# Input projections as seven half-size products for each pair of column blocks, and the program rewritten around such pairs

## The reference, cut to what matters

```python
for i in range(DEPTH):                                   # layer A, then layer B
    q, k, v, mq, gate = split_proj(x @ w_in[i], SPLIT)   # A: 5120 columns, B: 10240 columns
    o_mix = mixer_a(q, k, v, sink, pos) or mixer_b(q, k, v, pos)
    o_mem = memory_attention(mq, mem, w_mkv[i])          # 4 heads, 256 memory tokens
    y = concat([o_mix, o_mem]) * silu(gate)              # 1024 x 2048
    x = layer_norm(ALPHA * x + y @ w_out[i], ln_g[i], ln_b[i])
```

## Time and profile before

| | us |
|---|---|
| median of 3 runs | 2400.32 (2396.41 to 2400.34) |
| profiled execution | 2399.52 |
| its span, first to last instruction | 2397.7 |
| TensorE busy | 2320.9 (97%) |
| VectorE busy | 1375.1 (57%) |
| ScalarE busy | 997.1 (42%) |
| GpSimd busy | 269.4 (11%) |

### The profile page before, as it was taken

The page is one execution under the profiler, slowest core; times in us unless marked ns, Lnnn a source line. Parts: engine busy times, 40 slices in busy tenths (PEclk is TensorE's granted clock), DMA queues, the critical chain, the costliest instruction groups (busy, mean ns, idle before and its releaser), DMA issues.

```text
span 2397.7 us, 37763 instructions
## 1 busy us (share of the span) xinstructions
PE 2320.9 (97%) x11856; PEld 1943.2 (81%) x11856; DVE 1375.1 (57%) x3528; ACT 997.1 (42%) x2329; POOL 269.4 (11%) x214
## 2 busy tenths in 40 slices
PE   8999999999999989999999999999999999999996
PEld 7788888888888877887888788887887878888885
DVE  3455646565443755566565765656656666464375
ACT  4343434344442233443534435344354453444222
POOL 0001000000000221011011110111101111000022
PEclk9999999999999999999999999999999999999998
DMA  7211121211125531112022120221212112122543
GB/s 223 72 45 45 36 62 35 62 35 53 52 97 197 179 132 53 40 51 78 26 71 62 35 71 27 71 62 35 71 29 68 62 35 73 36 86 96 198 174 130
DMA packets 184656, 183.83 MB, mean 77 GB/s; under 512 B 16260, under 2 KB 156620, under 8 KB 183052
## 3 DMA queue, kind: packets, MB, share of 16 engines
q1 hardware_dynamic: 184588, 183.03, 23.9%
HBM read 157.39 MB, written 25.61 MB: 76 GB/s over the span
## 4 chain that ended last, share of the span: by engine, by line
PE 77%; DVE 12%; issue 4%; ACT 4%; DMA 1%; DVEq 0%; POOL 0%; SPq 0%; POOLq 0%; ACTq 0%
PE bank L857 15%; PE bank L859 15%; PE bank L858 15%; PE bank L919 7%; PE bank L894 6%; PE bank L984 5%; PE bank L990 4%; PE bank L988 4%; PE bank L907 4%; DVE work L1369 3%; DVE work L1465 2%; DVE work L1367 2%; DMA w_raw<-in_w_mkv 1%; DVE work L1372 1%; ACT w_split L1092 1%
## 5 line engine op out<-in xcount | busy, mean ns | idle before, releaser
L857 PE MATMUL bank<-xT,w_split 128*128 128x512 f32 (+1 forms) x2048 | 890.8, 435 | 12.8 <-DVE w_split L1337 6.5
L859 PE MATMUL bank<-xT,w_split 128*128 128x512 f32 (+1 forms) x2048 | 789.8, 386 | 0.0
L858 PE MATMUL bank<-xT,w_split 128*128 128x512 f32 (+1 forms) x2048 | 789.6, 386 | 0.0
L857 PEld LDWEIGHTS bank<-xT,w_split 128*128 128x128 f32 x2048 | 390.9, 191 | 75.8 <-DVE xT L1345 7.5
L859 PEld LDWEIGHTS bank<-xT,w_split 128*128 128x128 f32 x2048 | 386.7, 189 | 79.4
L858 PEld LDWEIGHTS bank<-xT,w_split 128*128 128x128 f32 x2048 | 391.4, 191 | 69.1 <-issue 23.5
L1337 DVE TENSOR_TENSOR w_split<-w_raw,w_split 128x1024 fp32r<-128x1024 f32 x200 | 257.4, 1287 | 326.1 <-ACT w_split L1092 163.2
L1125 ACT ACTIVATE work<-work,soft 128x256 f32<-128x256 f32 (+2 forms) x448 | 226.4, 505 | 389.2 <-DVE soft L1401 324.5
L788 POOL TENSOR_TENSOR work<-work,cosb 32x512 f32<-32x512 f32 x128 | 173.1, 1352 | 1421.1 <-ACT work L1182 1342.8
L1182 ACT COPY work<-bank 128x512 f32<-128x512 f32 x176 | 102.7, 584 | 399.0 <-PE bank L859 398.1
L919 PEld LDWEIGHTS bank<-work 128*128 128x128 f32 x1488 | 224.7, 190 | 33.5
(11 more groups left out here) (98 smaller groups left out, 2543.3 us busy)
## 6 DMA issues: line engine op xcount, KB each, us to landing
w_raw<-in_w_in_b SPq DMA_DIRECT2D x80, 512.0 KB, 3.8
w_raw<-in_w_out SPq DMA_DIRECT2D x64, 512.0 KB, 3.4
w_raw<-in_w_in_a SPq DMA_DIRECT2D x40, 512.0 KB, 3.9
work<-weight_scratch SPq DMA_DIRECT2D x12, 1536.0 KB, 6.5
y_scratch<-work SPq DMA_DIRECT2D x32, 512.0 KB, 3.1
y_raw<-y_scratch SPq DMA_DIRECT2D x64, 256.0 KB, 3.5
w_raw<-in_w_mkv SPq DMA_DIRECT2D x16, 512.0 KB, 4.4
work<-in_x SPq DMA_DIRECT2D x4, 1024.0 KB, 7.1
```

Source lines behind the costliest of these rows:

```text
L857: nc.tensor.matmul(dst, w_h, xT[:, 0, k, cols], start=(k == 0), stop=False)
L858: nc.tensor.matmul(dst, w_h, xT[:, 1, k, cols], start=False, stop=False)
L859: return nc.tensor.matmul(dst, w_l, xT[:, 0, k, cols], start=False, stop=(k == KT - 1))
```

## The change

The projection of a pair of column blocks (256 columns) for all 1024 tokens is a product of 2x2 blocks: token halves by halves of the contraction, times halves of the contraction by the two column blocks. Before, it takes eight block products, each 4 contraction steps. Now it takes seven (Winograd's form of Strassen's algorithm), of sums of the activations and sums of the weights:

- **Steps.** A pair is 28 steps, 7 products of 4, where two segments were 32 steps. There are 20 pairs in layer A and 40 in layer B, and the step is the same three matmuls.
- **Activations.** `x_ops` holds seven 512x512 operands, split, where `xT` held four. The sums are made from rows once for each layer (`token_sums`, VectorE and GpSimd), and 28 groups of transposes take the place of 16. In layer A, 24 of them stand in the memory projection; in layer B they stand before the first products (`X_BEFORE`).
- **Weights.** Four quarters of 128x512 are loaded for each pair and seven operands made of them: three sums on VectorE, one on GpSimd, seven casts and seven subtractions of 512 columns where there were two of each of 1024.
- **Results.** Products accumulate in the two banks `PB`: in the first bank the products 0, 2, 4 and 6 on top of each other, in the second 1 and 3, then 5. After the products 0, 1, 2 and 6 ScalarE copies the bank out, after 3, 4 and 5 VectorE adds it to what was copied. A product waits for the reader of the product two before it, since both use the same bank.
- **Riders.** A tile starts every second step, one job rides on one pair. Scores of layer A and of memory heads are plain float32 now. In layer B the normalisation of the tiles is gone (the denominators enter the mixing weights). The sine product is GpSimd's; the minimum of negated logits takes the place of the maximum, without the one-column operation behind it.
- **Mixing** in layer B is done by halves of the tokens, weights loaded by halves.
- **Output projection**: the same matmuls. The first tiles of y are loaded when all of y has been stored.
- The program has no loops.

The diff, cut to its core:

```diff
-STEPS = 2 * KT
-LEAD, LAG_T, LAG_PV = 3, 6, 8
+PRODUCTS = 7
+STEPS = 4 * PRODUCTS
+RAW, RING, AHEAD = 6, 4, 3
+LAG_MASK, LAG_EXP, LAG_NORM, LAG_T, LAG_PV, LAG_OUT = 1, 2, 3, 5, 7, 8
...
-        xT = sb("xT", [P, 2, KT, L], F32R)
-        w_split = sb("w_split", [P, 2, 2, D], F32R)
-        w_raw = sb("w_raw", [P, 2, D])
+        x_ops = sb("x_ops", [P, X_OPS * XW], F32R)
+        raw = sb("raw", [P, RAW, HALF])
+        sums = sb("sums", [P, 2, HALF])
+        ring = sb("ring", [P, RING, 2, HALF], F32R)
...
-            def step(dst, cols, slot, k):
-                w_h = w_split[:, slot, 0, k * P:(k + 1) * P]
-                w_l = w_split[:, slot, 1, k * P:(k + 1) * P]
-                nc.tensor.matmul(dst, w_h, xT[:, 0, k, cols], start=(k == 0), stop=False)
-                nc.tensor.matmul(dst, w_h, xT[:, 1, k, cols], start=False, stop=False)
-                return nc.tensor.matmul(dst, w_l, xT[:, 0, k, cols], start=False,
-                                        stop=(k == KT - 1))
+            def three_parts(dst, n, k, x_h, x_l, start, stop, again=False):
+                w_h = ring[:, n % RING, 0, k * P:(k + 1) * P]
+                w_l = ring[:, n % RING, 1, k * P:(k + 1) * P]
+                nc.tensor.matmul(dst, w_h, x_h, start=start, stop=False, skip_group_check=again)
+                nc.tensor.matmul(dst, w_h, x_l, start=False, stop=False, skip_group_check=again)
+                return nc.tensor.matmul(dst, w_l, x_h, start=False, stop=stop,
+                                        skip_group_check=again)
+                if j == 0 and not first:
+                    pe.wait_ge(c11_done, g)
+                if j == 1 and not first:
+                    pe.wait_ge(c21_done, g)
+                if j >= 2:
+                    pe.wait_ge((r1_done, r5_done, r2_done, c12_done, c22_done)[j - 2], g + 1)
+            def product_step(g, j, k):
+                dst = PB[(g + (j in (1, 3, 5))) % 2][:, :]
+                mm = three_parts(dst, stage_of(g, j), k, xs[:, j, 0, k, :], xs[:, j, 1, k, :],
+                                 start=(k == 0 and j in (0, 1, 5)),
+                                 stop=(k == KH - 1), again=True)
+                if k == KH - 1:
+                    mm.then_inc(prod, 1)
...
+        def x_source(j, i):
+            first, second = slice(0, HALF), slice(HALF, D)
+            return (rows[:, i, first], t1_rows[:, i, :], t2_rows[:, i, :], rows[:, 4 + i, second],
+                    t3_rows[:, i, :], rows[:, i, second], t1_rows[:, i, :])[j]
+        X_BEFORE = (((6,), (), (), (), (), (), ()),
+                    ((0,), (1, 2), (3,), (4,), (5, 6), (), ()))
...
+                if due is not None and due[1] < 3:
+                    (first_sum, second_sum, third_sum)[due[1]](due[0])
+            def first_sum(g):
+                if g > 0:
+                    dve.wait_ge(w_lo, stage_of(g - 1, 2) + 1)
+                    dve.wait_ge(s4_done, g)
+                nc.vector.tensor_tensor(sums[:, 0], quarter(g, 0), quarter(g, 1), ALU.add
+                                        ).then_inc(s1_done, 1)
+            def second_sum(g):
+                dve.wait_ge(w_lo, stage_of(g, 1) + 1)
+                nc.vector.tensor_tensor(sums[:, 0], sums[:, 0], quarter(g, 2), ALU.subtract
+                                        ).then_inc(s2_done, 1)
+            def third_sum(g):
+                dve.wait_ge(s1_done, g + 1)
+                nc.vector.tensor_tensor(raw[:, load_of(g, 0) % RAW], quarter(g, 2), quarter(g, 0),
+                                        ALU.subtract).then_inc(s3_done, 1)
+            def fourth_sum(g):
+                load = load_of(g, 3)
+                pool.wait_ge(s2_done, g + 1)
+                pool.wait_ge(raw_in[load % RAW], landed_value(load))
+                if g > 0:
+                    pool.wait_ge(w_lo, stage_of(g - 1, 3) + 1)
+                nc.gpsimd.tensor_tensor(sums[:, 1], raw[:, load % RAW], sums[:, 0], ALU.subtract
...
+            def summed(g, e, h, j, bank_, before, done):
+                dest = pairs[g].dests[e]
+                dve.wait_ge(*product_done(g, j))
+                dve.wait_ge(before, g + 1)
+                for view, take in dest.views(h):
+                    st = nc.vector.scalar_tensor_tensor(
+                        out=view, in0=take(bank_[:, :]), scalar=dest.factor,
+                        in1=take(r5) if e else view, op0=ALU.mult, op1=ALU.add)
...
+                    pair = pair_at(layer, T, 16)
+                    if pair is not None:
+                        summed(pair.g, 0, 1, 3, PB[1 - pair.g % 2], r2_done, c12_done)
+                    pair = pair_at(layer, T, 20)
+                    if pair is not None:
+                        if pair.g == FIRST_PAIR[1]:
+                            dve.wait_ge(rows_out, 16 * TILES)
+                        if pair.g == FIRST_PAIR[1] + 5:
+                            dve.wait_ge(spilled, 16)
+                        summed(pair.g, 1, 1, 4, PB[pair.g % 2], r5_done, c22_done)
+                    pair = pair_at(layer, T, 24)
+                    if pair is not None:
+                        summed(pair.g, 0, 0, 5, PB[1 - pair.g % 2], r1_done, c11_done)
+                    if T < STEPS and T % 4 == 0:
+                        for op in X_BEFORE[layer][T // 4]:
...
+                    pair = pair_at(layer, T, 4)
+                    if pair is not None:
+                        first_part(pair.g, 0, 0, r1_done)
+                    pair = pair_at(layer, T, 8)
+                    if pair is not None:
+                        fifth_part(layer, pair.g)
+                    pair = pair_at(layer, T, 12)
+                    if pair is not None:
+                        first_part(pair.g, 1, 2, r2_done)
+                    pair = pair_at(layer, T, STEPS)
+                    if pair is not None:
+                        last_part(pair.g)
...
+        if ropes == [0]:
+            self.ropes = [(0, 1, 17, 21), (0, 0, 25, 29)]
+        elif ropes == [0, 1]:
+            self.ropes = [(0, 1, 17, 20), (1, 1, 21, 24), (0, 0, 25, 28), (1, 0, 29, 32)]
...
-                nc.vector.stream_shuffle(b, v, swap).then_inc(rope_turned, 1)
-                dve.wait_ge(rope_turned, r + 1)
-                nc.vector.tensor_tensor(b, b, sin_h, ALU.mult).then_inc(rope_sine, 1)
-                dve.wait_ge(rope_sine, r + 1)
-                dve.wait_ge(rope_cosine, r + 1)
-                nc.vector.tensor_tensor(v, a, b, ALU.add).then_inc(rope_done, 1)
...
+                pool.wait_ge(rope_turned, rope_no[key] + 1)
+                for view, take in dest.views(h, ROPE):
+                    nc.gpsimd.tensor_tensor(view, view, take(cosb[:, h * HALF:(h + 1) * HALF]),
+                                            ALU.mult)
+                for view, take in turned_views(dest, h):
+                    mul = nc.gpsimd.tensor_tensor(view, view, take(sinb[:, h * HALF:(h + 1) * HALF]),
+                                                  ALU.mult)
+                mul.then_inc(rope_mul, 1)
...
+                dve.wait_ge(rope_mul, rope_no[key] + 1)
+                for (view, _), (b, _) in zip(dest.views(h, ROPE), turned_views(dest, h)):
+                    add = nc.vector.tensor_tensor(view, view, b, ALU.add)
+                add.then_inc(rope_done, 1)
...
-                load_w(0, 0, 0)
-                load_w(0, 0, 1)
-                for j in range(3):
-                    sp.wait_ge(stored[j], 16 * totals[j] + (16 if j > 0 else 0))
-                load_y(0, 0, 0)
-                load_y(0, 0, 1)
-                store(0, NE - 1, (G_MA, G_MB)[layer] + MEM_HEADS - 1)
+                for name in stored:
+                    if stores_after[layer][name]:
+                        sp.wait_ge(stored[name], 16 * stores_after[layer][name])
+                sp.wait_ge(*product_done(FIRST_PAIR[layer] + PAIRS[layer] - 1, 2))
+                load_y(0, 0)
+                load_y(0, 1)
...
-                (q_h, q_l), (k_h, k_l) = ([qk_split[:, w, part, at[w]:at[w] + size]
-                                           for part in range(2)] for w, size in ((0, P), (1, n)))
-                nc.tensor.matmul(dst, q_h, k_h, start=True, stop=False)
-                nc.tensor.matmul(dst, q_h, k_l, start=False, stop=False)
-                nc.tensor.matmul(dst, q_l, k_h, start=False, stop=True).then_inc(s_ready, 1)
+                nc.tensor.matmul(SB[count % 2][:, 0:size], q, k, start=True, stop=True
+                                 ).then_inc(s_ready, 1)
...
+                        if layer == 1 and T == 0:
+                            for i in range(4):
+                                token_sums(1, i)
+                                second_token_sums(1, i)
...
+                    if due is not None and due[0].whole:
+                        normalise(layer, *due)
...```

```

(1 more changed line is left out.)

2277 lines of the change are left out of this document (1244 added, 1033 removed).

## The result

The changed kernel takes **2403.55 us** (median of 10 runs, 2400.97 to 2408.88) against 2399.86 for the kernel before (10 runs): ratio 1.0021, 95% interval 1.0013 to 1.0030. The forecast was 2284, a gain. The 240 steps are gone, and nothing is gained.

What follows compares the result with a forecast made beforehand. TensorE's own pace was taken as the bound. The terms -163.2 + 17 - 6 + 20 + 26 - 9 made -115.2 us, giving 2284 us; forecast 2255 to 2315 (chance 0.60), whole range 2235 to 2350.

Steps and rivals of the forecast that it cites:

- Step 1: Projections on TensorE: 1920 steps become 1680, 240 steps of 0.68 us taken away, -163.2 us.
- Step 2: Scores of layer A and of memory: plain ones dearer than split ones, 0.67 against 0.54 at 384 columns, +17 us.
- old waits: Waits inside the layers of the kernel before: some 55 us, 24 idle in layer B, the rest estimated.
- Step 3: Start: most transpose groups stand in the memory projection where TensorE waited for weights, -6 us.
- Step 4: Change of layers: sums and transposes before layer B's first products, 46 us lost against 25, +20 us.
- Step 5: End of each layer: first load of y waits for the last store, 13 us a layer, +26 us for two.
- Step 6: Waits inside the layers: 46 us against some 55 before, -9 us; ends -45 and +75.
- The prediction's own test: Forecast wrong if a head's period is over 96 us or under 88, or idle time within layers passes 100 us.
- rival B: Bank additions late because VectorE waits at line 1634 for GpSimd: 1 us per addition, 180 additions, 2464 us; chance 0.05.
- A: VectorE stands still for all GpSimd work, level with TensorE per head: +5 us per head, 2344 us; chance 0.18.
- C: Waits inside the layers all gone, gaps at change and ends of layers at their low ends: 2235 us; chance 0.13.
- D: Instructions streamed from DRAM without loops, about 120 blocks each stopping TensorE 1 us: 2400 us; chance 0.04, shared with under-delivery.

Runs made afterwards that it cites:

- e6: Changed kernel with both rotary products on VectorE, each in its own step, and layer B's rotary work of two of a head's three pairs moved later: 2271.69 us.
- e8: Changed kernel with the first two y tiles loaded within the last pair and later ones ahead of weight loads and residual transfers: 2381.54 us.
- e9: e6 with e8's earlier y loads, first two y tiles split inside the last pair, and residual, norm and mask transfers not in one burst: 2232.33 us.
- e1: Changed kernel with the sine and cosine products of the rotary halves left out of the computation: 2271.84 us.
- e4: Changed kernel with the sine product on VectorE right behind the turn, the cosine product staying on GpSimd: 2376.09 us.
- e5: Changed kernel, both products still on GpSimd; layer B's turns of two of a head's three pairs moved later, the rest at e2's places: 2323.56 us.
- e2: Changed kernel, same instructions, with all six rotary additions of the schedule and three of the turns at later steps: 2356.93 us.
- e3: Changed kernel with both rotary products issued by VectorE just before the addition of line 1634 instead of by GpSimd: 2331.34 us.

## Why the prediction was wrong

- **Step 1, projections (-163.2):** right in the pace, 0.68 us a step where nothing rides on it.
- **Step 2, scores (+17):** wrong in sign when taken singly. A plain 384-column score adds 1.12 - 0.68 = 0.44 us in the median step, under the 0.54 of the split one it replaces, and not 0.67; a 256-column one adds 0.34. But steps with three blocks of transposes and value products are dearer than before, 1.85 us in the median against 1.65. Together the term came to about nothing.
- **Steps 1, 2 and the old waits together.** Against the kernel almost without waits (e6) the layers are 45 and 139 us shorter than before, 184 together; forecast without waits was 163.2 - 17 + 55 = 201. Of the 55 us of old waits the trace of the kernel before shows about 26 as idle time of TensorE (3.4 of 609 us in layer A, 23.0 of 1295 in layer B), and e6 itself still has about 5. The rest of the 184, some 163 us, is work, where the forecast had 146.
- **Step 3, start (-6):** -8.5. **Step 4, change of layers (+20):** +22. **Step 5, ends (+26):** +20. Right, by the steps given: ScalarE waited for the load of y before each pause ended. (1 us for semaphores and 1.5 of slow clock were put into step 5 with no row of their own.)
- **Left out: the output projections, +21.** The prediction takes the output projections as unchanged and never asks what is queued ahead of a y load in SyncE's order. In the changed kernel a y load stands behind weight loads that wait for a free slot and, once, behind six transfers (8.32 us at 719.08). e8 and e9 gave back 12 and 19 of the 21 us.
- **Step 6, waits inside the layers (-9, end +75): the step that failed.** It allows 3 us per head in layer B and 0.5 per pair in A, 46 us. With the turns moved and both products on VectorE (e6) layer B takes 124 us less and layer A 14: 138 us that the places and the engine of the change cost, 124 of them in the layer for which 36 were allowed. 138 - 46 + 17 + 21, less 7 for steps 3 to 5 (-2.5, +2, -6), makes 123; the forecast was 123.5 under the profiled execution. (The prediction's last sum is 1 us short: 2282.5 + 1.8 + 0.8 is 2285.) The prediction's own test, a head over 96 us, was met with 97.5.

Why did step 6 fail? Its load for VectorE looks right by luck: 64% was worked out for a head (58 us in 90), and the page says 64% for the whole span. In layer B VectorE was busy for 662.94 of 1000 us, 64.6 us per head: 6.6 more than worked out, in a longer period. Without the GpSimd products (e1) the same operations took 644.68 of 1000, 56.3 us per head. So the list was good, and what GpSimd adds to it was left out. The main error was to ask a mean for something that a burst decides: e6 loads VectorE with 786 of 1000 us, and TensorE doesn't wait. Step 6 names the places where VectorE's list is long, "between 16 and 24", and then allows a flat 3 us. VectorE has no gap from 1454.4 to 1466.8, GpSimd none from 1460.8 to 1469.7, and the addition of line 1634 stands where both queues are full. The two products were priced at 1.35 each with a weight sum between (rival B), and took 1.6 to 1.7 in the mean. The mixing product, which line 1016 puts ahead of them on GpSimd at this place of a head, was in no list of what the addition waits for, and took 3.79 us here; but the head's other long wait came without it.

**The rivals.** *A (engines in turn, 2344)* had its 5 us per head from the load of both engines summed. The mechanism is there (e4, and rows like 1465.13 above), but at the most it is worth the 2.0 us per head between e5 and e6, or 5.3 in the order of the change; both figures also hold the waits between the engines. *B (slower than before, 2464)* named the place, line 1634, and the reason, standing in order for GpSimd. It named the wrong victim: TensorE waits 3.3 us for bank additions in the whole run, and as the prediction said, they stand in front of the addition of line 1634; the next masks stand behind it. The question left unasked was when TensorE needs each thing in that queue, masks as well as bank additions. Where additions were moved, as in e2, bank additions did come late. *C (2235)* is almost what the mended kernel takes (2232.33), by another road. *D (instruction streaming)*: 91 blocks on queue 8 instead of the 120 expected, and e6 shows TensorE busy for 999.35 of 1000 us with as many; it costs nothing that can be seen.

The rule weighed in the prediction (the Trainium skill, SBUF — State Buffer, "SBUF: two separate sides": while one of the two engines has the shared ports, "the other fully blocks") agrees in its direction with the rows again: in the mean 2.27 us (e4) for a product that took 1.35 in the kernel before. But all of GpSimd's time added to VectorE's is not what happened: in the changed kernel GpSimd is busy for 688.9 us, 432 more than in e1, and VectorE for 119 more.

**The clock's part** is worked out, not shown by a run of its own. Per head the changed kernel loses 10.5 us against e6, and 7.4 of them are TensorE's waits for masks; the other 3 fit stretches like the one at 0.59 behind the wait of 3.62 us (a window granted at 0.96 instead of 1.00 is 3.9 us in 97.5). The longer waits go with the lower clock: in 1000:2000 the longest wait and the granted clock are 0.5 us and 1.00 (e6), 1.6 and 1.00 (e2), 2.4 and 0.99 (e3), 2.9 and 0.96 (e4), 3.6 and 0.96 (the change). The relation is not strict. In e2 the clock falls for a few microseconds behind one wait of 1.63 us (at 1086.75), and in the changed kernel it stays at 1.00 in 1112:1124, behind waits of 2.90 and 1.46:

```profile
1087.00:1091.00 4.00, 4.00 (x11) 2.98 (x12) 4.00 (x9) 2.57 (x9) 1.80 (x1) 0.60 0.00 0
```

**What stays open:** how the loss in the changed kernel splits between the lengthened operations of the two engines and the order they stand in (no run keeps the order and the engines and removes the lengthening); how it splits between the mixing product and the two rotary products; and whether the 16.8 us at the change of layers can go, which wasn't tried.

## What to carry to other kernels

An engine at 64% can still be the bound: list what stands in its queue behind every wait on another engine, and when the critical engine needs each item. Handing work to an idle engine needs slack on both sides of the hand-over; here doing it oneself (0.76 us a product in e6) was cheaper than a wait for it. And when a large cut of work moves the time by nothing, move the order before giving up the cut: in this case later places for the rotary turns and additions were worth 2% (e2), and order and engine together 5.5% (e6).

## What the runs showed of the hardware

- A GpSimd product of 32 x 512 takes 1.6 to 1.7 us in the mean of the changed kernel and 2.27 in e4, where the mean before was 1.35; single ones take 3.0. A mixing product of 128 x 512 took 3.79 (1462.46), with a mean of 2.76 over 24. VectorE's 0.68 us operations beside them take 1.05 to 2.03, and the same list of VectorE operations takes 1542.7 us with the products on GpSimd and 1424.0 without them.
- At the places of the change, giving GpSimd one of the two products (e4, 2376) was slower than giving it none (e3, 2331), and faster than giving it both (2403.55).
- A wait of TensorE can cost more than its length: after 3.62 us of standing came 7 us of work at a granted clock of 0.59, and over a head some three more microseconds. One wait of 1.63 us was followed by a fall too, and not every wait of 2.9 us was.
- A program of 32,000 instructions without a loop fetched 1.49 MB of them in 91 blocks on one queue and 0.57 MB in 70 packets on another. In e6, with as many, TensorE was busy for 999.35 of 1000 us.
